# Attention couples stored in whole rows, placed by loads of squares, and gated by VectorE

## The chip, the core and the metric

The kernel runs on one core of one Trainium2 chip. A core has five instruction streams: TensorE (PE in the profile, PEld for its weight loads), VectorE (DVE), ScalarE (ACT), GpSimd (POOL) and SyncE (SP), which here only issues DMAs. Each stream runs its instructions in the order in which they were written and waits for semaphores where it is told to. The metric is device time in microseconds. The kernel before took 924.09 us (median of three runs, 919.69 to 927.16).

## The reference, cut to what matters

One decoder layer on 1024 rows of width 1024, in float32:

```python
h = rms_norm(x, pre_norm)
proj = h @ w_in                      # q, k, v, gate_a, u, v_b, gate_b, mg_a, mg_b
o_a = sliding_window_attention(q, k, v, sinks, rel_bias)   # 16 heads of 64, window 128
y_a = (o_a * silu(gate_a)) @ w_branch_a
o_b = spatial_gating(gelu(u), gelu(v_b), ...)
y_b = (o_b * silu(gate_b)) @ w_branch_b
out = (sigmoid(mg_a) * y_a + sigmoid(mg_b) * y_b) @ w_out
x = x + rms_norm(out, post_norm)
```

The change touches what lies between the softmax of the attention and the product `o_a * silu(gate_a)`. For each head and each block of 128 queries the probabilities (128 queries by 2 x 128 keys, folded into one 128 x 128 tile) have to be transposed, so that TensorE can multiply them with the values.

## The kernel before, in words

Matrices are multiplied in pieces of high and low parts (`w_hi`, `w_lo`; three matmuls for one product), and in seven products in place of eight per pair of column blocks. After a first stage (normalisation, `v_b`, keys and values; to about 137 us) come 24 pairs of column blocks, `n` = 0 to 23. Each has seven steps `s`, with one product of 12 matmuls in each. Attention is woven into steps of pairs 1 to 17: `attention_all(n, s)` turns a step into a head pair `p` (0 to 7) and a step `k` of it. A head pair begins every 14 steps and is done after 22, so that its last 8 steps lie beside the first 8 of the next. Below, "step 0" to "step 13" are the places in this period of 14 steps (about 50 us); step 16 of one head pair is step 2 of the period.

A head pair has 8 query blocks, and two blocks make a **couple** (c = 0 to 3). A couple's four 128 x 128 probability tiles lie side by side in `prob[j % 2]` (j = 4p + c). They are transposed in two parts: VectorE transposes 32 x 32 squares in place (L2143), and two sets of DMAs carry the tile out to DRAM and back, which puts the squares in their places. The stations of a couple, by the step k = 3c + lag at which each stream reaches them:

- lag 3, SP: `prob_away` stores the couple, four DMAs (L666).
- lag 4, SP: `prob_back` loads it into `turned_in`, one DMA (L675). It waits for the stores, and for GpSimd to have read the couple before out of `turned_in` (`pool_own`).
- lag 7, ACT: `turned_hi` copies it to `pt_pack` (high part, L1590).
- lag 8, POOL: the low part (L1859) and the masked copy `pt_prev` (L1864), which lets the values go.
- lag 9, PE: `values`, eight matmuls (L1073), in the middle of the step's product.
- lag 10, ACT and DVE: ACT copies two quarters of the result (L1607, L1608) to `o_tmp`, DVE adds the other two (L2149, L2150).
- lag 11, POOL: the product with the gate (L1873). SP stores the gate's row at k = 15 and 21 (L687).

In each step a stream does the attention first (`attend`) and then its part of the pair (`after`). For pair n + 1 ScalarE makes the high parts of its loaded columns (`left_hi`: L1364 for the first raw block, L1383 for half of the second, L1371 and L1378 for sums), GpSimd the low parts (`left_lo`, L1816) and the sums (L1881, L1882, L1888, L1890). SP loads the raw columns (`load_pair`, L542) at steps 5, 6, 12 and 13; they share its queue with the attention's DMAs and with the stores of the merge gates (L699).

Of the kernel before, what the change touches and what calls it, by code (L numbers as in the profile page):

```python
# [5 lines left out]
P = 128  # L6
# [13 lines left out]
HEAD_PAIRS = N_HEADS // 2  # L20
# [122 lines left out]
def build(nc, x, rel_bias, pre_norm, post_norm, w_in, sinks, sgu_ln_g, sgu_ln_b,  # L143
          w_spatial, b_spatial, w_branch_a, w_branch_b, w_out, out):
    f32 = mybir.dt.float32
# [19 lines left out]
    v_d = nc.dram_tensor("v_d", [P, 2 * NT * P], i32)  # L165
    prob_d = nc.dram_tensor("prob_d", [4 * HEAD_PAIRS, 4, P, P], f32)
    bias_d = nc.dram_tensor("bias_d", [N_HEADS, BIAS_ROW], f32)
    skew_d = nc.dram_tensor("skew_d", [N_HEADS, P, BIAS_ROW], f32)

    with ExitStack() as ctx:  # L170
# [340 lines left out]
        def _(sp):  # L511
# [150 lines left out]
            def prob_away(j):  # L662

                sp.wait_ge(turn_ok, 2 * j + 2)
                for q in range(4):
                    sp.dma_start(prob_d[j, :, :, :].rearrange("c (g a) (q b) -> q a c g b", g=4, q=4)[q],  # L666
                                 prob[j % 2][32 * q:32 * (q + 1), 1:1 + 4 * P].rearrange("a (c g b) -> a c g b", c=4, g=4)
                                 ).then_inc(prob_out[j % 2], 16)

            def prob_back(j):  # L670

                sp.wait_ge(prob_out[j % 2], 64 * (j // 2 + 1))
                if j:
                    sp.wait_ge(pool_own, POOL_FRONT + j)
                sp.dma_start(turned_in.rearrange("p (c x) -> p c x", c=4), prob_d[j, :, :, :].rearrange("c p x -> p c x")).then_inc(prob_in, 16)  # L675

            def attend(p, k):
                for c in couple_at(k, 3):
                    prob_away(4 * p + c)
                for c in couple_at(k, 4):  # L680
                    prob_back(4 * p + c)
                if k == 11 and p + 1 < HEAD_PAIRS:
                    load_bias(p + 1)
                if k in (15, 21):
                    h = k // 21
                    sp.wait_ge(og_ok, 4 * p + 2 * h + 2)
                    sp.dma_start(ga_d[bass.ds(p, 1), :, h * HALF:(h + 1) * HALF].rearrange("a p s -> p (a s)"),  # L687
                                 gate_w(p, h)).then_inc(ga_out[h], 16)
# [527 lines left out]
        def _(act):  # L1216
# [347 lines left out]
            def exps(p, blk):  # L1564
# [5 lines left out]
                if s % 2 == 0 and s >= 4:  # L1570
                    act.wait_ge(prob_out[s // 2 % 2], 64 * (s // 4))
                for h in range(2):
# [11 lines left out]
            def turned_hi(j):  # L1584
                act.wait_ge(prob_in, 16 * (j + 1))
                if j:
# [5 lines left out]
            def attend(p, k):  # L1592
# [4 lines left out]
                if k == 2 and p + 1 < HEAD_PAIRS:  # L1597
                    act.dma_start(*skew(p + 1)).then_inc(bias_out, 16)
                for c in couple_at(k, 7):
                    turned_hi(4 * p + c)  # L1600
                for g in couple_at(k, 10):
# [83 lines left out]
            for n in range(1, PAIRS):  # L1685
                for s in range(7):
                    for at in attention_all(n, s):
                        attend(*at)
                    after(n, s)
            def after_tile(f, i):  # L1690

# [27 lines left out]
        def _(pool):  # L1719
# [126 lines left out]
            def attend(p, k):  # L1846
# [9 lines left out]
                for c in couple_at(k, 8):  # L1856
# [5 lines left out]
                    if j:  # L1862
# [4 lines left out]
                        base=-1, pattern=[[0, 8], [-1, P]], channel_multiplier=1).then_inc(pt_ok, 1)  # L1867
                for g in couple_at(k, 11):
                    if g == 0:
                        pool.wait_ge(gate_ok, 2 * p + 2)  # L1870
                    part = gate_w(p, g // 2)[:, g % 2 * 256:(g % 2 + 1) * 256]
                    pool.wait_ge(oadd_ok, 4 * p + g + 1)
                    nc.gpsimd.tensor_tensor(part, o_tmp, part, ALU.mult).then_inc(og_ok, 1)  # L1873

# [55 lines left out]
        def _(dve):  # L1930
# [184 lines left out]
            def attend(p, k):  # L2115
# [29 lines left out]
                for g in couple_at(k, 10):  # L2145
# [4 lines left out]
                    nc.vector.tensor_tensor(o_tmp[64:128, :], o[64:128, 256:512], o_tmp[64:128, :],  # L2150
                                            ALU.add).then_inc(oadd_ok, 1)

            def u_mix(n):
# [441 lines left out]
```

## Time and profile before

| | us |
|---|---|
| median of three runs | 924.09 (919.69 to 927.16) |
| the profiled execution | 923.55 |
| its span, first to last instruction | 921.8 |
| PE busy | 893.6 (97%) |
| DVE, ACT, POOL busy | 629.0, 509.3, 532.4 |
| granted TensorE clock, mean | 0.993 |

The profile is of one execution. A PE that is busy 97% of the span is pipelined matmuls end to end; what is not matmul is to be looked for in its gaps. The other engines are busy for 55 to 68% of the span, but each only in its own order.

### The profile page before, as it was taken

What the parts mean: (1) busy time and instruction counts of PE and PEld (TensorE: products, weight loads), DVE (VectorE), ACT (ScalarE), POOL (GpSimd) and SP (SyncE); (2) the same over time, 40 slices, a digit from 0 to 9 for tenths busy, and PEclk for the clock granted to TensorE, in tenths of its full rate; (3) what the DMA queues carried; (4) which work ended last, traced back from release to release, by engine and by line L of the source; (5) the groups of instructions that cost most, each with busy time, mean ns of one, the idle gap of its engine ahead of it and who ended that gap; (6) DMA issues with size and microseconds to landing.
All of it is one profiled execution on the core that took longest, in us unless ns stands there. A gap on an engine that the chain in (4) does not pass through costs nothing.

```text
span 921.8 us, 12475 instructions
## 1 busy us (share of the span) xinstructions
PE 893.6 (97%) x4204; PEld 742.8 (81%) x4204; DVE 629.0 (68%) x1135; ACT 509.3 (55%) x982; POOL 532.4 (58%) x395
## 2 busy tenths in 40 slices
PE   9999999989999998989899999999999999999997
PEld 7888888878787877778787877888888888888886
DVE  6776794536455554445463679789679878989968
ACT  6654355766767676657577684344443534434563
POOL 3564237678878878687778868454452142042236
PEclk9999999999999999999999999999999999999999
DMA  8886645363645556644536474533369650335004
GB/s 298 201 198 161 230 164 149 112 158 87 165 113 143 133 145 169 181 125 112 144 93 168 115 202 141 183 103 105 101 230 372 197 205 1 118 113 225 0 1 183
DMA packets 211472, 139.29 MB, mean 151 GB/s; under 512 B 91320, under 2 KB 180432, under 8 KB 211280
## 3 DMA queue, kind: packets, MB, share of 16 engines
q1 hardware_dynamic: 209168, 135.05, 49.8%
q10 hardware_dynamic: 2240, 3.43, 1.1%
q8 instruction: 34, 0.56, 0.3%
q14 instruction: 30, 0.25, 0.1%
HBM read 98.06 MB, written 43.54 MB: 154 GB/s over the span
## 4 chain that ended last, share of the span: by engine, by line
PE 71%; POOL 9%; ACT 6%; DVE 5%; DMA 4%; issue 4%; SPq 2%; ACTq 0%; POOLq 0%; DVEq 0%
PE acc L1033 27%; PE acc L1205 11%; PE acc L886 10%; PE ps_m L1205 7%; PE ps_t L1205 7%; DMA raw<-in_w_in 4%; PE acc L976 2%; PE ps_m L1073 2%; POOL w_lo L1816 2%; PE ps_t L1050 1%; POOL pt_pack L1859 1%; SPq L666 1%; ACT soft L1573 1%; POOL pt_prev L1864 1%; DVE soft L2134 1%
## 5 line engine op out<-in xcount | busy, mean ns | idle before, releaser
L1033 PE MATMUL acc<-mv,w_hi 128*128 128x512 f32 x1344 | 348.1, 392 | 2.9 <-ACT c L1423 1.5
L1033 PEld LDWEIGHTS acc<-mv,w_hi 128*128 128x128 f32 x1344 | 247.1, 189 | 52.4 <-issue 6.3
L1033 PE MATMUL acc<-mv,w_lo 128*128 128x512 f32 x672 | 181.0, 391 | 0.0
L1816 POOL TENSOR_TENSOR w_lo<-sums,w_hi 128x1024 fp32r<-128x1024 f32 x48 | 117.0, 2439 | 85.1 <-ACT w_hi L1371 55.0
L1033 PEld LDWEIGHTS acc<-mv,w_lo 128*128 128x128 f32 x672 | 127.4, 190 | 27.8
L1816 POOL TENSOR_TENSOR w_lo<-raw,w_hi 128x1024 fp32r<-128x1024 f32 (+1 forms) x48 | 94.4, 1967 | 43.9 <-ACT w_hi L1364 32.4
L1205 PE MATMUL acc<-right,left 128*128 128x512 f32 x432 | 98.7, 389 | 0.0
L1205 PEld LDWEIGHTS acc<-right,left 128*128 128x128 f32 x432 | 81.0, 188 | 17.2 <-DVE left L2194 0.4
L2149 DVE TENSOR_TENSOR soft<-ps_m,soft 64x256 f32<-64x256 f32 x32 | 13.3, 416 | 103.8 <-ACT soft L1608 103.8
L1573 ACT ACTIVATE soft<-soft,neg_max 128x129 f32<-128x129 f32 x128 | 50.5, 396 | 55.3 <-DVE neg_max L2134 55.2
L886 PE MATMUL acc<-mv 128*128 128x512 f32 x288 | 69.3, 395 | 0.0
L1205 PE MATMUL ps_t<-right,left 128*128 128x512 f32 x288 | 67.2, 389 | 0.0
L1205 PE MATMUL ps_m<-right,left 128*128 128x512 f32 x288 | 67.2, 389 | 0.0
L2143 DVE STREAM_TRANSPOSE soft<-soft 128x128 f32<-128x128 f32 x128 | 32.3, 292 | 50.8 <-ACT soft L1581 50.6
L1581 ACT ACTIVATE soft<-soft,inv_den 128x128 f32<-128x128 f32 x128 | 44.3, 393 | 34.9 <-DVE inv_den L2123 34.9
L1205 PEld LDWEIGHTS ps_t<-right,left 128*128 128x128 f32 x288 | 54.1, 188 | 11.2
L1205 PEld LDWEIGHTS ps_m<-right,left 128*128 128x128 f32 x288 | 54.1, 188 | 11.2
L886 PEld LDWEIGHTS acc<-mv 128*128 128x128 f32 x288 | 53.4, 188 | 11.4 <-ACT mv L1238 0.3
L1859 POOL TENSOR_TENSOR pt_pack<-soft,pt_pack 128x512 fp32r<-128x512 f32 x32 | 41.9, 1309 | 19.6 <-ACT pt_pack L1590 19.6
L1073 PE MATMUL ps_m<-pt_pack,v_st 128*128 128x256 f32 x128 | 27.1, 305 | 17.6 <-POOL pt_prev L1864 17.6
L1073 PEld LDWEIGHTS ps_m<-pt_pack,v_st 128*128 128x128 f32 x128 | 21.1, 198 | 25.5 <-POOL pt_prev L1864 24.0
L2134 DVE CUSTOM_DVE_ANT_0 soft<-ps_t,bias_t,sink_b 128x128 f32<-128x128 f32 x128 | 39.9, 350 | 2.1
(282 smaller groups left out, 1661.5 us busy)
## 6 DMA issues: line engine op xcount, KB each, us to landing
raw<-in_w_in SPq DMA_DIRECT2D x56, 512.0 KB, 5.3
prob_d<-soft SPq DMA_DIRECT2D x128, 64.0 KB, 3.5
soft<-prob_d SPq DMA_DIRECT2D x32, 256.0 KB, 3.1
ht_d<-sums SPq DMA_DIRECT2D x8, 512.0 KB, 5.2
mix_d<-mix_b SPq DMA_DIRECT2D x8, 512.0 KB, 3.8
ga_d<-gate SPq DMA_DIRECT2D x16, 256.0 KB, 4.6
tb<-tb_d SPq DMA_DIRECT2D x4, 1024.0 KB, 5.3
ub<-mix_d SPq DMA_DIRECT2D x7, 512.0 KB, 3.5
```

The source lines that it names most:

```text
L886: ins = nc.tensor.matmul(acc[b][:, hf * HALF:(hf + 1) * HALF], left, right, start=(m < 2), stop=(m >= 46), skip_group_check=True)
L976: ins = nc.tensor.matmul(acc[b][:, hf * HALF:(hf + 1) * HALF], (w_lo if x == 2 else w_hi)[:, w], right, start=(m < 2), stop=(m >= 46), ski ...
L1033: ins = nc.tensor.matmul(bank, (w_lo if y == 2 else w_hi)[:, left + k * P:left + (k + 1) * P], right[:, (OPW if y == 1 else 0) + k * HALF: ...
L1073: ins = nc.tensor.matmul(o, v_st[:, v0:v0 + P], pt[:, y * 512:(y + 1) * 512].rearrange("p (x c) -> p x c", x=4)[:, heads, :], start=(kb == ...
L1205: ins = nc.tensor.matmul(bank, l[:, c:c + P], r[:, (OPW if y == 1 else 0) + k * HALF:(OPW if y == 1 else 0) + (k + 1) * HALF], start=(m == ...
L1573: ins = nc.scalar.activation(exp_w(s, h), neg_w(blk, h), ACT.Exp, scale=-1.0, bias=neg_max[:, head(blk, h)], accum_out=row_sum[:, head(blk ...
L1581: ins = nc.scalar.activation(w, w, ACT.Copy, scale=inv_den[:, head(blk, h)])
L1816: nc.gpsimd.tensor_tensor(w_lo[:, c], src, w_hi[:, c].bitcast(f32), ALU.subtract).then_inc(wlo_ok, 1)
L1859: nc.gpsimd.tensor_tensor(pt_pack[:, 512:1024], turned_in, pt_pack[:, 0:512].bitcast(f32), ALU.subtract).then_inc(pool_own, 1)
L2134: ins = nc.vector.tensor_tensor_reduce(out=neg_w(blk, h)[:, 1 - h:1 - h + P], in0=bank[:, h * 256 + P:(h + 1) * 256], in1=bias_t[:, bias:b ...
L2143: ins = nc.vector.transpose(w, w)
L2149: own.link(nc.vector.tensor_tensor(o_tmp[0:64, :], o[0:64, 0:256], o_tmp[0:64, :], ALU.add))
```

## The change

`prob_d` now has one row of 512 numbers for each of 128 partitions. `prob_away` stores a couple with one DMA of whole rows (2 KB each), and `prob_back` loads it with four, one for each group of 32 partitions, whose pieces are rows of squares (32 numbers, 128 bytes): the squares are placed on the way back and not on the way out. `prob_back` moves from lag 4 to lag 5, and the gate's stores from k = 15 and 21 to 14 and 20. On ACT `turned_hi` keeps its lag of 7 but now stands behind `after` of its step, where it stood ahead of the copies and of `after`. The product with the gate is made by VectorE at lag 10, right behind the addition, and no longer by GpSimd at lag 11.

```diff
-    prob_d = nc.dram_tensor("prob_d", [4 * HEAD_PAIRS, 4, P, P], f32)
+    prob_d = nc.dram_tensor("prob_d", [4 * HEAD_PAIRS, P, 4 * P], f32)
...
-                for q in range(4):
-                    sp.dma_start(prob_d[j, :, :, :].rearrange("c (g a) (q b) -> q a c g b", g=4, q=4)[q],
-                                 prob[j % 2][32 * q:32 * (q + 1), 1:1 + 4 * P].rearrange("a (c g b) -> a c g b", c=4, g=4)
-                                 ).then_inc(prob_out[j % 2], 16)
+                sp.dma_start(prob_d[j, :, :], prob[j % 2][:, 1:1 + 4 * P]).then_inc(prob_out[j % 2], 16)
...
-                sp.wait_ge(prob_out[j % 2], 64 * (j // 2 + 1))
+                sp.wait_ge(prob_out[j % 2], 16 * (j // 2 + 1))
                 if j:
                     sp.wait_ge(pool_own, POOL_FRONT + j)
-                sp.dma_start(turned_in.rearrange("p (c x) -> p c x", c=4), prob_d[j, :, :, :].rearrange("c p x -> p c x")).then_inc(prob_in, 16)
+                for g in range(4):
+                    sp.dma_start(turned_in[32 * g:32 * (g + 1), :].rearrange("a (c q b) -> a c q b", c=4, q=4),
+                                 prob_d[j, :, :].rearrange("(q a) (c g b) -> g a c q b", q=4, c=4, g=4)[g]).then_inc(prob_in, 16)
...
-                for c in couple_at(k, 4):
+                for c in couple_at(k, 5):
                     prob_back(4 * p + c)
...
-                if k in (15, 21):
-                    h = k // 21
+                if k in (14, 20):
+                    h = k // 20
...
-                for c in couple_at(k, 7):
-                    turned_hi(4 * p + c)
...
                     after(n, s)
+                    for p, k in attention_all(n, s):
+                        for c in couple_at(k, 7):
+                            turned_hi(4 * p + c)
...
-                for g in couple_at(k, 11):
-                    if g == 0:
-                        pool.wait_ge(gate_ok, 2 * p + 2)
-                    part = gate_w(p, g // 2)[:, g % 2 * 256:(g % 2 + 1) * 256]
-                    pool.wait_ge(oadd_ok, 4 * p + g + 1)
-                    nc.gpsimd.tensor_tensor(part, o_tmp, part, ALU.mult).then_inc(og_ok, 1)
...
+                    dve.wait_ge(oadd_ok, gg + 1)
+                    if g == 0:
+                        dve.wait_ge(gate_ok, 2 * p + 2)
+                    part = gate_w(p, g // 2)[:, g % 2 * 256:(g % 2 + 1) * 256]
+                    nc.vector.tensor_tensor(part, o_tmp, part, ALU.mult).then_inc(og_ok, 1)
```

Three places show how instructions move (the lines of the changed kernel are one to six lower). The first is ScalarE's order at step 2 of the period, where the fourth couple (c = 3) is turned. Before:

```order
L1456 ACTIVATE ev<-ev 128x512
L1590 ACTIVATE pt_pack<-soft 128x512
L1607 ACTIVATE soft<-ps_m 64x256
L1608 ACTIVATE soft<-ps_m 64x256
L1581 ACTIVATE soft<-soft,inv_den 128x128 x2
L1598 DMA skew_d<-bias_d 256x1x384
L1451 ACTIVATE ev<-ev 128x512
L1383 ACTIVATE w_hi<-raw 128x512
```

and now:

```order
L1455 ACTIVATE ev<-ev 128x512
L1604 ACTIVATE soft<-ps_m 64x256
L1605 ACTIVATE soft<-ps_m 64x256
L1580 ACTIVATE soft<-soft,inv_den 128x128 x2
L1597 DMA skew_d<-bias_d 256x1x384
L1450 ACTIVATE ev<-ev 128x512
L1382 ACTIVATE w_hi<-raw 128x512
L1589 ACTIVATE pt_pack<-soft 128x512
```

The copy to `pt_pack` has gone from the head of this stretch to its end. The second place is ScalarE at step 7, where the first couple (c = 0) is turned. Before:

```order
L1573 ACTIVATE soft,row_sum<-soft,neg_max 128x129 x2
L1590 ACTIVATE pt_pack<-soft 128x512
L1468 ACTIVATE ev<-ev 128x512
L1364 ACTIVATE w_hi<-raw 128x1024
L1581 ACTIVATE soft<-soft,inv_den 128x128 x2
```

and now:

```order
L1572 ACTIVATE soft,row_sum<-soft,neg_max 128x129 x2
L1467 ACTIVATE ev<-ev 128x512
L1363 ACTIVATE w_hi<-raw 128x1024
L1589 ACTIVATE pt_pack<-soft 128x512
L1580 ACTIVATE soft<-soft,inv_den 128x128 x2
```

Here two instructions come between, and the second of them reads a raw block from DRAM. The third place is SP's order over steps 3 to 6 (with what each DMA waits for). Before:

```order
L666 DMA prob_d<-soft 32x16x32 [waits turn_ok]
L666 DMA prob_d<-soft 32x16x32 x3
L675 DMA soft<-prob_d 128x4x128 [waits pool_own,prob_out0]
L699 DMA tb_d<-c 128x512 [waits mt_ok]
L542 DMA raw<-in_w_in 128x8x128 [waits wlo_ok,sum_ok]
```

and now:

```order
L665 DMA prob_d<-soft 128x512 [waits turn_ok]
L673 DMA soft<-prob_d 32x16x32 [waits pool_own,prob_out0]
L673 DMA soft<-prob_d 32x16x32 x3
L698 DMA tb_d<-c 128x512 [waits mt_ok]
L542 DMA raw<-in_w_in 128x8x128 [waits wlo_ok,sum_ok]
```

The load of the first raw block still stands behind the couple's round trip; what was four DMAs and one is now one and four. Behind it (step 6) the next couple's stores, four before and one now, stand ahead of the second raw block's load.

## Rows read from the trace of the kernel before

**Rows 1.** The page: engines by busy us, share of the span, instructions.

```profile
PE   893.6 (97%) x4204; PEld 742.8 (81%) x4204; DVE 629.0 (68%) x1135; ACT 509.3 (55%) x982; POOL 532.4 (58%) x395
```

**Rows 2.** Waits: who waited for whom, us in total, times, longest.

```profile
PE ps_m L1073 <- POOL pt_prev L1864: 17.6, 15, 2.8
```

**Rows 3.** Timeline, PE's values, couples 1, 3, 0, 1 (start, us, [idle before]).

```profile
251.12 0.51 PE L1073 MATMUL ps_m<-pt_pack,v_st 128*128 128x256 f32 x2 [1.53 <-POOL pt_prev L1864]
...
421.08 0.40 PE L1073 MATMUL ps_m<-pt_pack,v_st 128*128 128x256 f32 x2
...
437.76 0.74 PE L1073 MATMUL ps_m<-pt_pack,v_st 128*128 128x256 f32 x4 [0.50 <-POOL pt_prev L1864]
...
450.46 0.68 PE L1073 MATMUL ps_m<-pt_pack,v_st 128*128 128x256 f32 x2 [2.41 <-POOL pt_prev L1864]
```

**Rows 4.** Timeline of GpSimd between the first couple and the second.

```profile
441.58 1.30 POOL L1881 TENSOR_TENSOR sums<-raw 128x512 f32<-128x512 f32 x1 [1.51 <-issue]
```

**Rows 5.** Timeline of ScalarE at step 2, fourth couple.

```profile
415.47 0.62 ACT L1590 ACTIVATE pt_pack<-soft 128x512 fp32r<-128x512 f32 x1
...
418.04 0.40 ACT L1581 ACTIVATE soft<-soft,inv_den 128x128 f32<-128x128 f32 x1 [1.14 <-DVE inv_den L2123]
...
419.22 0.62 ACT L1383 ACTIVATE w_hi<-raw 128x512 fp32r<-128x512 f32 x1
```

**Rows 6.** Timeline of ScalarE at step 7, first couple.

```profile
434.08 0.62 ACT L1590 ACTIVATE pt_pack<-soft 128x512 fp32r<-128x512 f32 x1
434.60 0.62 ACT L1468 ACTIVATE ev<-ev 128x512 f32<-128x512 f32 x1
436.25 1.06 ACT L1364 ACTIVATE w_hi<-raw 128x1024 fp32r<-128x1024 f32 x1 [1.04 <-DMA raw<-in_w_in]
```

**Rows 7.** Timeline, third couple, GpSimd idle till ScalarE's copy: ScalarE, GpSimd, PE.

```profile
254.97 0.63 ACT L1590 ACTIVATE pt_pack<-soft 128x512 fp32r<-128x512 f32 x1
...
257.05 1.09 POOL L1864 TENSOR_SCALAR_AFFINE_SELECT pt_prev<-pt_pack 128x1024 fp32r<-128x1024 f32 x1
...
260.82 0.40 PE L1073 MATMUL ps_m<-pt_pack,v_st 128*128 128x256 f32 x2
```

**Rows 8.** Timeline, fourth couple three head pairs earlier: ScalarE, then PE.

```profile
265.32 0.62 ACT L1590 ACTIVATE pt_pack<-soft 128x512 fp32r<-128x512 f32 x1
...
270.93 0.40 PE L1073 MATMUL ps_m<-pt_pack,v_st 128*128 128x256 f32 x2
```

**Rows 9.** Chain of waits (start, us): PE behind the second couple and the third.

```profile
450.46 1.96 PE ps_m L1073 x8
452.43 6.31 PE acc L1033 x24
...
461.93 0.95 PE ps_m L1073 x8
...
463.35 5.46 PE acc L1033 x24
```

**Rows 10.** Windows: length, busy of PE, PEld, DVE, ACT, POOL, clock, DMA, GB/s.

```profile
451.00:453.00 2.00, 2.00 (x9) 1.89 (x9) 0.00 (x0) 0.00 (x0) 2.00 (x2) 0.50 1.09 272
252.00:254.00 2.00, 2.00 (x11) 1.68 (x11) 0.00 (x0) 0.25 (x1) 2.00 (x1) 1.00 1.13 261
```

**Rows 11.** Timeline of SP's queue: the raw blocks' loads of steps 5 and 6.

```profile
430.34 0.38 SPq L542 DMA_DIRECT2D raw<-in_w_in  x1
...
435.99 0.40 SPq L542 DMA_DIRECT2D raw<-in_w_in  x1
```

**Rows 12.** Lines of DVE: duration ns min/median/max, first and last start.

```profile
L2109 DVE SCALAR_TENSOR_TENSOR gate<-c x8: 681/1508/1532, 163.8 to 509.8; 128x512 f32<-128x512 f32 x8
...
L2149 DVE TENSOR_TENSOR soft<-ps_m,soft x32: 407/417/419, 196.4 to 572.4; 64x256 f32<-64x256 f32 x32
```

**Rows 13.** DMA issues: count, KB each, median us from issue to landing.

```profile
prob_d<-soft SPq DMA_DIRECT2D x128, 64.0 KB, 3.5
...
ta_d<-ev SPq DMA_DIRECT2D x8, 256.0 KB, 2.0
```

More of the change, by code:

```diff
@@ L1570, in exps @@
                 if s % 2 == 0 and s >= 4:
-                    act.wait_ge(prob_out[s // 2 % 2], 64 * (s // 4))
+                    act.wait_ge(prob_out[s // 2 % 2], 16 * (s // 4))
                 for h in range(2):
@@ L1584, in turned_hi @@
             def turned_hi(j):
-                act.wait_ge(prob_in, 16 * (j + 1))
+                act.wait_ge(prob_in, 64 * (j + 1))
                 if j:
```

## The prediction

> **What bounds the kernel now.** Read the page first. PE is busy for 893.6 us, 97% of the span of 921.8 [rows 1], so at most 28.2 us are to be had from waits, and what matters is what PE waits for. The waits name one thing: PE stood 17.6 us in 15 waits before the values of the attention, for GpSimd's `pt_prev` [rows 2]. The timeline of PE shows where. In each period of 14 steps the first couple (c = 0) waits some 0.5 us and the second (c = 1) 1.5 to 2.4 us; the fourth (c = 3) does not wait, and neither does the third [rows 3]. Over the eight head pairs I take 3.3 us for the first couples (six of 0.50 to 0.53 and one of 0.16), 0.8 us for the last fourth couple, and so 13.5 us for seven second couples.
>
> Two more things are needed. First, from the first couple's values to the point at which PE wants the second's is 10.3 us (450.46 − 2.41 − 437.76), whereas GpSimd was on its way from the one to the other for 12.7 us, of which it stood 1.51 us at L1881 until a raw block had landed [rows 3, 4]. Its own work there is thus 11.2 us, 0.9 us more than PE leaves it: of a second couple's wait 0.9 us is GpSimd's work, and the rest is the late load. Second, in the chain of waits PE takes 1.96 us for eight values matmuls and 6.31 us for the 24 behind them after a wait of 2.41 us, where the third couple shows 0.95 and 5.46 [rows 9]: 1.9 us lost again. The windows show why. The granted clock is 0.50 behind that wait, the 1.2 GHz level, and 1.00 behind one of 1.53 us [rows 10]. Three of the seven second couples waited 2.4 us or more: 3 x 1.9 = 5.6 us.
>
> **ScalarE's order.** This is the part with a cost. ScalarE's time of the turned copy stands at a fixed distance from PE: in the fourth couple 5.61 us before the values, at 415 us as at 265 us [rows 3, 5, 8]. So I can reckon each couple alone. From the start of the copy to the end of `pt_prev`, where GpSimd has nothing else to do, it takes 3.17 us (257.05 + 1.09 − 254.97) [rows 7].
>
> Fourth couple. The copy began at 415.47 and PE wanted the values at 421.08: 2.4 us to spare. Now it comes behind L1383, which ended at 419.84 [rows 5]. The copy's own 0.62 us is gone from ahead of it, and VectorE's product comes into the path, since the reciprocal for which L1581 waits [rows 5] stands behind it on DVE. The product is 128 x 256. It costs at least the 0.42 us of the addition L2149, and at most the 1.51 us of L2109, which is twice as wide; I take 0.5, the nearest in size being L2149 [rows 12]. The copy begins at 419.6, `pt_prev` ends at 422.8, and PE waits 1.7 us where it waited not at all. Eight times this is 13.6 us, less the 0.8 us of the last one before: **+12.8 us**.
>
> First couple. The copy began at 434.08; PE was ready at 437.26 and waited 0.50 us [rows 3, 6]. Now L1468 and L1364 come first: 0.52 + 0.97 us as they overlap, if the raw block is there. The copy begins at 435.57, `pt_prev` ends at 438.74, and PE waits 1.48 us. Eight times is 11.8 less 3.3: **+8.5 us**.
>
> Second couple. The copy now stands behind the two small copies and one eviction; GpSimd, with its 11.2 us of work, comes to it at about the same time. Third couple: the two small copies and L1378 come first, and PE takes the values 5.85 us after the old start of the copy (260.82 − 254.97) [rows 7], of which 3.17 are needed. **0** for both, with a few tenths open for the second.
>
> **The round trip.** A couple's 256 KB went out in four DMAs of 64 KB in pieces of 128 bytes, 3.5 us to landing each. Whole rows of 2 KB are what the store of `ta_d` makes of the same 256 KB: 2.0 us [rows 13]. The way back takes over the 2048 small pieces, which no row shows for this tensor; by the nearest, the old stores, 3.5 us after the last issue, with 2.0 us as the lower end. `prob_back` leaves a step later (3.6 us, 199.3 us between two second couples over 56 steps [rows 3]), yet ScalarE wants the couple later too, by 1.5 us in the first couple and 4.1 in the fourth. I cost it at 0 on the couple's own path. Its cover is the distance from lag 5 to the end of lag 7; where that is gone, all later instructions on ScalarE stand behind `prob_in`.
>
> What the trip gives is on SP's queue. The first raw load (430.34) stood behind a `prob_back` that waited for slow stores, the second (435.99) behind four stores [rows 11]. Now the first stands behind four loads, but the store ahead lands sooner; the second behind one store. I take the second raw block to land before GpSimd is at L1881 (2 us or more earlier, where 1.51 was missing). Each second couple then waits only GpSimd's own 0.9 us: 8 x 0.9 = 7.2 in place of 13.5, **−6.3 us**. No wait is then over 1.7 us, and the clock stays up: **−5.6 us**.
>
> **The gate.** GpSimd loses 32 products, yet in the stretch that sets the second couple's wait, from one `pt_prev` to the next, it made none: 0. VectorE's product at steps 10, 13 and 5 stands ahead of a reciprocal as well, but there ScalarE's two copies now come 0.6 us earlier or the path has slack of over 1 us: 0. Behind the waiting DVE stand c22, the q parts and the transposes, none of which PE waits for within a step.
>
> A rule speaks against this part. The row first: L2109, with both inputs in SBUF, takes 0.68 us at its quickest and 1.51 at the median, while GpSimd is at work beside it [rows 12]. The Trainium skill, in "SBUF — State Buffer", section "Who interferes with whom", says that a VectorE instruction with two SBUF inputs shares an exclusive lock with GpSimd's reads, and that the other "fully blocks". By it the product could stand for one whole GpSimd instruction. The sum takes the product at 0.5 because GpSimd has just ended its sums at step 2 and now stands until the copy comes.
>
> **Sum.** 12.8 + 8.5 − 6.3 − 5.6 = +9.4 us on the profiled execution's 923.55: **933 us**. That execution lies 0.5 us under the median of the runs, 924.09, which changes nothing at this precision. About 1% is what a measurement of this kernel can tell from no change, that is 915 to 933.
>
> **Rivals.** (1) *The copies' places don't matter* and only the gains remain: 923.55 − 6.3 − 5.6 = 912 us, faster. It holds if ScalarE, no longer held by late loads, runs ahead of PE by more than 1.7 us. For it: ScalarE is busy for 55% of the span. Against it: the fixed 5.61 us, which the late load of one period and not of another left alone. (2) *One of the two new waits is covered*, most likely the first couple's (924 us, +0.9) or the fourth's (920 us): no change. Half a microsecond less on the path, or GpSimd's work in front of `pt_prev` in place of ScalarE, would do it for part. (3) *The raw block is late for ScalarE.* Before, L1364 stood 1.04 us for it, and nobody else did, because the turned copy was ahead [rows 6]. Now the copy is behind it, so each microsecond by which that load is late goes to PE, eight times. With the same 1.04 us: 933 + 8 = 941 us; from about 2 us on, the wait exceeds 2.4 us and 1.9 us of low clock are added each time. (4) *VectorE's product is held* for 1.5 us where I took 0.5: 8 us, 941 us. By the page's rule, one whole GpSimd subtraction, the same mechanism would show a product of over 2 us. (5) *The clock falls behind the new waits*: 1.7 us lies between 1.53, where it stayed, and 2.41, where it fell. At the eight fourth couples that is 8 x 1.9 = 15 us, 948 us. (6) *The stores don't get quicker* since what slows them is other traffic; the second couple's 6.3 and the clock's 5.6 us are not gained: 945 us.
>
> **Chances.** The forecast (927 to 939) 0.45; rivals 3 to 6 together (939 to 950) 0.23; rival 2 (919 to 927) 0.17; rival 1 (909 to 917) 0.15. The range leaves out most of rival 1 and the far end of 3 to 6: 915 to 945. Slower by over 1% (above 933) is half of the forecast and all of 3 to 6: 0.46. Within 1%: the other half and rival 2: 0.39. Faster by over 1%: 0.15.
>
> **What would show it.** In the profile after: PE's values of fourth couples with a wait of 1.7 us, first couples with 1.5, second couples with 0.9, all named as GpSimd's; GpSimd's L1859 waiting for ScalarE's copy at fourth couples by over 3 us; L1881 without a wait for its load; no window at clock 0.50 in the attention; the gate's product on DVE at 0.4 to 0.6 us. I would be wrong if the copy's distance to PE's values has grown at steps 2 or 7 by other ways than its place, if `prob_in` holds ScalarE, or if L1881 still waits.

## The result and the profile after

The changed kernel took 952.7 us (median of four runs, 951.8 to 955.8) beside 925.6 for the kernel before (919.7 to 928.7): a ratio of 1.0306, 95% interval 1.0248 to 1.0365. It is slower by 3%. The forecast was 933, with a range of 915 to 945: the direction was right, but the size was a third of what came, and the result lies outside the range. The two profiled executions took 923.55 and 952.93 us, 29.4 apart where 9.4 were forecast.

The page of the changed kernel, engines by busy us, share and instructions (against [rows 1]):

```profile
PE   903.0 (95%) x4204; PEld 750.7 (79%) x4204; DVE 644.5 (68%) x1167; ACT 508.0 (53%) x982; POOL 510.0 (54%) x363
```

The same 4204 matmuls are busy for 9.4 us longer. The work is the same, and the windows below show the granted clock at half in more stretches. The rest is waiting. The waits of the changed kernel (against [rows 2]):

```profile
PE ps_m L1072 <- POOL pt_prev L1864: 38.8, 23, 2.4
```

So there are 38.8 us of waits for `pt_prev` where there were 17.6. The time in which PE is not busy at all (span less busy) went from 28.2 to 48.2 us, and 20.0 + 9.4 make the 29.4. The timeline of PE's values, fourth couple, first, second, fourth (start, us, [idle before]):

```profile
388.19 0.50 PE L1072 MATMUL ps_m<-pt_pack,v_st 128*128 128x256 f32 x2 [1.94 <-POOL pt_prev L1864]
...
407.40 0.74 PE L1072 MATMUL ps_m<-pt_pack,v_st 128*128 128x256 f32 x4 [1.34 <-POOL pt_prev L1864]
...
418.74 0.51 PE L1072 MATMUL ps_m<-pt_pack,v_st 128*128 128x256 f32 x2 [1.21 <-POOL pt_prev L1864]
...
441.12 0.51 PE L1072 MATMUL ps_m<-pt_pack,v_st 128*128 128x256 f32 x2 [2.42 <-POOL pt_prev L1864]
```

The fourth couples wait 2.40 to 2.43 us six times and 1.94 once (1.7 forecast), the last not at all; the first 1.18 to 2.27 (1.48 forecast); the second 0.99 to 1.23 (0.9 forecast); the third not at all. The path to the last of these rows is best read from the end. ScalarE, VectorE and GpSimd before 441.12:

```profile
435.81 0.40 ACT L1580 ACTIVATE soft<-soft,inv_den 128x128 f32<-128x128 f32 x1 [1.48 <-DVE inv_den L2117]
...
437.52 0.62 ACT L1589 ACTIVATE pt_pack<-soft 128x512 fp32r<-128x512 f32 x1
```

```profile
427.97 2.62 DVE L2103 SCALAR_TENSOR_TENSOR gate<-c 128x512 f32<-128x512 f32 x1
430.51 0.15 DVE L2117 RECIPROCAL inv_den<-row_sum 128x2 f32<-128x2 f32 x1
...
435.28 0.42 DVE L2150 TENSOR_TENSOR gate<-soft,gate 128x256 f32<-128x256 f32 x1
435.62 0.16 DVE L2117 RECIPROCAL inv_den<-row_sum 128x2 f32<-128x2 f32 x1
...
438.10 0.69 DVE L2103 SCALAR_TENSOR_TENSOR gate<-ev 128x512 f32<-128x512 f32 x1
```

```profile
427.63 2.41 POOL L1816 TENSOR_TENSOR w_lo<-sums,w_hi 128x1024 fp32r<-128x1024 f32 x1
430.00 2.85 POOL L1816 TENSOR_TENSOR w_lo<-raw,w_hi 128x1024 fp32r<-128x1024 f32 x1
...
438.21 1.70 POOL L1859 TENSOR_TENSOR pt_pack<-soft,pt_pack 128x512 fp32r<-128x512 f32 x1 [2.87 <-ACT pt_pack L1589]
```

ScalarE's copy (L1589) starts 1.18 us before PE is ready (441.12 − 2.42 = 438.70). Beside its new place, which was the forecast's reason, three things make it and what follows late. The product (L2150) takes 0.42 us ahead of a reciprocal, and ScalarE waits 1.48 us for that where it was 1.14 [rows 5]: this was foreseen. GpSimd's L1859 takes 1.70 us where it takes 1.29 elsewhere, with VectorE's `gate<-ev`, two inputs in SBUF, beside it: this was not. And `gate<-c` takes 2.62 us. It starts 0.34 us behind a GpSimd subtraction and ends 0.55 us after it (427.97 + 2.62 = 430.59; 427.63 + 2.41 = 430.04).

The same trace has one fourth couple, at 388.19, ahead of which `gate<-c` is not held:

```profile
375.44 0.68 DVE L2103 SCALAR_TENSOR_TENSOR gate<-c 128x512 f32<-128x512 f32 x1
```

There the product starts 3.91 us before PE is ready and not 3.43, and the wait is 1.94 us and not 2.42: the held `gate<-c` is worth 0.48 us of each such wait.

The clock behind the waits, in windows of the changed kernel (columns as in [rows 10]):

```profile
460.70:463.70 3.00, 3.00 (x9) 2.32 (x9) 2.60 (x8) 1.49 (x6) 3.00 (x3) 0.50 0.76 223
441.40:443.40 2.00, 2.00 (x16) 1.87 (x16) 0.50 (x2) 0.00 (x0) 2.00 (x2) 1.00 0.13 51
```

It is at 0.50, the 1.2 GHz level, in nine stretches of 3.4 us in the attention, where the kernel before had three. Four of them begin within 1.3 us of a fourth couple's wait (1.94 to 2.42 us) and five at a first couple's (1.79 to 2.27); behind the wait of 2.42 us at 441 the clock stayed at 1.00, as behind two more of that size. The round trip's loads land after 2.7 us, inside the forecast's 2.0 to 3.5. Its stores land after 3.4 us where 2.0 were forecast. It never held ScalarE here. DMA issues: count, KB each, median us to landing (against [rows 13]):

```profile
prob_d<-soft SPq DMA_DIRECT2D x32, 256.0 KB, 3.4
soft<-prob_d SPq DMA_DIRECT2D x128, 64.0 KB, 2.7
```

### The profile page after: what moved, and what is told of

The parts are those of the page before. It is cut to its first block, busy times and chain, and to the rows that moved or that the text cites. A ratio compares the mean times of both kernels' runs of the same rounds, so it can differ in the third digit from the quotient of the medians.

```text
span 951.2 us, 12475 instructions
## 1 busy us (share of the span) xinstructions
PE 903.0 (95%) x4204; PEld 750.7 (79%) x4204; DVE 644.5 (68%) x1167; ACT 508.0 (53%) x982; POOL 510.0 (54%) x363
## 3 DMA queue, kind: packets, MB, share of 16 engines
q10 hardware_dynamic: 2240, 3.43, 1.0%
## 4 chain that ended last, share of the span: by engine, by line
PE 63%; POOL 14%; issue 9%; ACT 6%; DVE 5%; DMA 2%; SPq 1%; POOLq 0%; ACTq 0%; DVEq 0%
PE acc L1032 21%; PE acc L1204 10%; PE acc L885 9%; PE ps_m L1204 7%; PE ps_t L1204 7%; POOL w_lo L1816 5%; POOL pt_pack L1859 3%; POOL pt_prev L1864 3%; PE acc L975 2%; PE ps_m L1072 2%; DMA raw<-in_w_in 2%; PE ps_t L1049 2%; ACT soft L1572 1%; ACT w_hi L1370 1%; DVE soft L2128 1%
## 5 line engine op out<-in xcount | busy, mean ns | idle before, releaser
L1032 PEld LDWEIGHTS acc<-mv,w_hi 128*128 128x128 f32 x1344 | 249.7, 190 | 47.7 <-issue 0.3
L1032 PE MATMUL acc<-mv,w_lo 128*128 128x512 f32 x672 | 184.3, 397 | 0.0
L1032 PEld LDWEIGHTS acc<-mv,w_lo 128*128 128x128 f32 x672 | 129.9, 193 | 28.8
L1859 POOL TENSOR_TENSOR pt_pack<-soft,pt_pack 128x512 fp32r<-128x512 f32 x32 | 45.4, 1419 | 66.7 <-ACT pt_pack L1589 66.7
L1072 PE MATMUL ps_m<-pt_pack,v_st 128*128 128x256 f32 x128 | 28.0, 312 | 38.8 <-POOL pt_prev L1864 38.8
L2125 DVE COPY_PREDICATED ps_t<-before,ps_t 128x256 f32<-128x256 int32 x56 | 23.8, 425 | 59.8 <-PE ps_t L1049 59.4
```

The source lines that it names most:

```text
L1032: ins = nc.tensor.matmul(bank, (w_lo if y == 2 else w_hi)[:, left + k * P:left + (k + 1) * P], right[:, (OPW if y == 1 else 0) + k * HALF: ...
L1072: ins = nc.tensor.matmul(o, v_st[:, v0:v0 + P], pt[:, y * 512:(y + 1) * 512].rearrange("p (x c) -> p x c", x=4)[:, heads, :], start=(kb == ...
L1859: nc.gpsimd.tensor_tensor(pt_pack[:, 512:1024], turned_in, pt_pack[:, 0:512].bitcast(f32), ALU.subtract).then_inc(pool_own, 1)
L2125: own.link(nc.vector.copy_predicated(blocks(bank)[:, :, 1, :], before_i, blocks(bank)[:, :, 0, :]))
```

## The experiments

Times are medians; each ratio is to the kernel before on the same chip, with its 95% interval. Each trace is of one execution, and the clock differs between executions of one kernel (mean 0.979 to 0.985 in the change's four). "Ahead" and "behind" are the places of ScalarE's copy.

### The three parts one by one

**a3_trip_only**: kernel before with the new round trip alone. 

> The kernel before with the new trip alone (whole rows out, squares placed by four loads, a step later); copy at its old place, product on GpSimd, gate's stores at their old steps. Theory: the second raw block no longer holds GpSimd's sums, 912 to 918 us, within 3 us of the kernel that has the product on VectorE as well. Rival (trip costs): slower than 924 us.

**b1_copy_behind**: kernel before with the copy behind `after`. 

> The kernel before with ScalarE's turned copy behind the step's own work and nothing else changed. Theory: this alone makes it slower than the full change or as slow, 948 to 962 us: fourth couples wait some 1.6 us (no VectorE product ahead of the reciprocal), first couples 1.8 us and up to 1 us more since the raw block is still late for L1364, second couples 1.5 us and more, and the clock falls in most periods. Rival (the order is covered, trip or gate is the cost): within 5 us of the kernel before.

**b2_gate_vector**: kernel before with the product on VectorE. 

> The kernel before with the product with the gate on VectorE behind its addition and nothing else changed. Theory: the product takes 0.43 us and is off the path; GpSimd had no product in the stretch that makes PE wait, so within 3 us of the kernel before (921 to 928 us). Rival (gate is the cost): 935 us or more.

**a1_copy_ahead**: changed kernel with one part undone:

```diff
+                for c in couple_at(k, 7):
+                    turned_hi(4 * p + c)
                 for g in couple_at(k, 10):
...
                     after(n, s)
-                    for p, k in attention_all(n, s):
-                        for c in couple_at(k, 7):
-                            turned_hi(4 * p + c)
```

> The changed kernel with ScalarE's turned copy back at its old place, ahead of the copies of the values and of the step's own work; trip and gate as changed. Theory (ScalarE's order is the cost): fourth couples wait for nothing, first couples 0.5 us, second couples 0.9 to 1.2 us, the clock does not fall in the attention; 912 to 918 us, faster than the kernel before. Rival (the trip with loads of squares is the cost): the copy waits for prob_in, and the time stays at 940 us or more. Rival (VectorE's product is the cost): also 940 or more, with the waits of VectorE's reciprocal longer.

| | us | ratio |
|---|---|---|
| before | 924.8 | |
| trip | 917.1 | 0.9899 (0.987 to 0.9929) |
| copy behind | 939.1 | 1.013 (1.0079 to 1.0181) |
| product on VectorE | 935.5 | 1.0095 (1.0051 to 1.0139) |
| trip + product (a1) | 933.1 | 1.0084 (1.0059 to 1.011) |
| trip + copy behind + product (the change) | 952.7 | 1.0306 (1.0248 to 1.0365) |

The trip alone is faster, the copy costs 14 us, and the product on VectorE, which the forecast had at 0 on its own, costs 11 to 16. The expectations that rested on a free product (a1, b2, and a3's "within 3 us" of a1) fell. So did b1's 948 to 962: its fourth couples wait 1.61 us, as expected, but most of its first couples 1.18 and not 1.8, its second couples 1.04 and not 1.5, and the clock falls twice. Two of its first couples wait 2.85 and 4.44 us, where ScalarE stood 1.59 and 3.18 us for the raw block just before. Where the product's price arises is seen in b2 at step 5, VectorE and GpSimd:

```profile
277.86 1.01 DVE L2150 TENSOR_TENSOR gate<-soft,gate 128x256 f32<-128x256 f32 x1
278.80 0.15 DVE L2117 RECIPROCAL inv_den<-row_sum 128x2 f32<-128x2 f32 x1
```

```profile
276.20 2.40 POOL L1816 TENSOR_TENSOR w_lo<-sums,w_hi 128x1024 fp32r<-128x1024 f32 x1 [2.42 <-ACT w_hi L1371]
```

The product ends at 278.87, 0.27 us after GpSimd's subtraction (278.60); ScalarE waits 2.07 us for the reciprocal where it waited 1.14, and the first couple's copy starts 1.53 us before PE is ready where a3 shows 3.16.

### Is it the place, or what VectorE reads?

**a7_product_psum**: a1 with another input of the product. It leaves the addition out of what is multiplied, so that one input lies in PSUM.

```diff
-                    nc.vector.tensor_tensor(part, o_tmp, part, ALU.mult).then_inc(og_ok, 1)
+                    nc.vector.tensor_tensor(part, o[:, 0:256], part, ALU.mult).then_inc(og_ok, 1)
...
-                    pe.wait_ge(oadd_ok, g - 1)
+                    pe.wait_ge(og_ok, g - 1)
```

> As the kernel with the copy ahead and the product on VectorE behind the addition (933.1), but the product reads the first 256 columns of the values' bank in PSUM in place of o_tmp, so that one input lies in SBUF and one in PSUM; TensorE waits for the product before it writes that bank again. (What is computed is changed: it multiplies the gate with numbers before the addition.) Theory A with the lock of two SBUF inputs: the products take 0.42 us each and not 1.0 at the mean (32.0 us in all), the normalisation at step 5 waits 1.5 us in place of 2.07, and the time lies between 917 and 933, about 924. Rival E, the product is long for another reason (its place, its shape): 32 us of products, and 933.

It took 918.5 us, 0.9934 (0.9905 to 0.9963), which leaves 1.4 us (by the ratios 3) of the 16 between a1 and a3. VectorE's group of products in a1, then in a7 (busy us, mean ns):

```profile
L2149 DVE TENSOR_TENSOR gate<-soft,gate 128x256 f32<-128x256 f32 x32 | 32.0, 999 | 1.1
```

```profile
L2149 DVE TENSOR_TENSOR gate<-ps_m,gate 128x256 f32<-128x256 f32 x32 | 13.6, 424 | 1.1
```

And at step 5 of a7 the product stands in the middle of the same subtraction of GpSimd and takes 0.42 us (VectorE, GpSimd):

```profile
425.50 0.42 DVE L2149 TENSOR_TENSOR gate<-ps_m,gate 128x256 f32<-128x256 f32 x1
```

```profile
423.83 2.40 POOL L1815 TENSOR_TENSOR w_lo<-sums,w_hi 128x1024 fp32r<-128x1024 f32 x1 [2.42 <-ACT w_hi L1370]
```

So a VectorE instruction of two SBUF inputs stands until GpSimd's ends, and one of the same size with one input in PSUM doesn't. With the copy ahead this is nearly the whole price of the product. The length of a held one is regular: in the kernel before, the change, b2, a1, a5, a6, a10 and a13, each of the 117 products of over 0.9 us ends 0.27 to 0.29 us after the GpSimd instruction beside which it started, and each of the 25 such `gate<-c` 0.55 us after it.

**a8_sum_in_psum** makes the whole computation in this way: the additions write to PSUM.

```diff
-                    own.link(nc.vector.tensor_tensor(o_tmp[0:64, :], o[0:64, 0:256], o_tmp[0:64, :], ALU.add))
-                    nc.vector.tensor_tensor(o_tmp[64:128, :], o[64:128, 256:512], o_tmp[64:128, :],
+                    own.link(nc.vector.tensor_tensor(o[0:64, 0:256], o[0:64, 0:256], o_tmp[0:64, :], ALU.add))
+                    nc.vector.tensor_tensor(o[64:128, 0:256], o[64:128, 256:512], o_tmp[64:128, :],
```

> Copy ahead, new round trip, product on VectorE behind the addition; but the addition leaves its result in PSUM (the first 256 columns of the values' bank) and the product reads it there, with the gate in SBUF: the whole computation is made, and no product has two inputs in SBUF. TensorE waits for the product before it writes that bank again. Theory A with the lock: like the kernel whose product read PSUM without the sum, 918.5, so 916 to 921, products of 0.42 us each, none longer. Rival F: writing sums to PSUM or holding the bank for the product makes TensorE wait: 925 or more.

921.6 us, 0.997 (0.9948 to 0.9991), products of 0.42 us: the mechanism as expected, the time at the end of its range. Its first couples wait 1.21 us.

**a6_ahead_late** (a1 with the product at the end of VectorE's step) and **a5_product_late** (the same on the changed kernel):

```diff
                     after(n, s)
+                    for p, k in attention_all(n, s):
+                        for g in couple_at(k, 10):
...
+                            nc.vector.tensor_tensor(part, o_tmp, part, ALU.mult).then_inc(og_ok, 1)
```

> The changed kernel with ScalarE's copy ahead as before and VectorE's product at the end of VectorE's step. The same with the product behind the addition took 933.1, and with the product on GpSimd 917.1. Theory A: ScalarE's normalisation at step 5 waits 1.14 us again and not 2.07, the first couples' copy is 3.1 us before PE's values and not 1.53, their waits go from 2.14 to about 0.5 us: 8 x 1.6 = 13 us less and 3 stretches at low clock (6 us), 916 to 921. Rival D, load or port wherever it stands: 930 to 935.

> The changed kernel with VectorE's product moved from behind the addition to the end of VectorE's step (behind its part of the pair). Theory A: the reciprocal comes 0.37 us earlier, so the fourth couples wait 2.0 in place of 2.42 us; gate<-c still takes 2.6 us, because GpSimd's work is where it was. With 8 x 0.37 = 3 us less and the falls of the clock behind these waits partly gone (up to 8 us), 941 to 950. Rival D, it is the mere load on VectorE or the shared port, wherever the product stands: 952 +- 3.

a6: 925.0 us, 0.9977 (0.9947 to 1.0007), a gain over a1 of half of what was expected: its first couples still wait 1.75 us, and its products are still long (25.9 us in all), only in another place. a5: 940.7 us, 1.0149 (1.0096 to 1.0201), with fourth couples at 2.2 us and `gate<-c` at 2.9. Neither theory's numbers hold for a6. Place and lock seem to pay a part each; a6 does not separate them, since the late product is held too.

**a12_psum_late**: a8 with the product at the end of the step. 

> As the kernel before in this list, with the product at the end of VectorE's step. In the one with the product behind the addition, the first couples waited 1.02 us where they wait 0.5 with the product on GpSimd; theory A says that this is the product's own 0.42 us ahead of the reciprocal, so that it goes: 0.5 us at each of 7 first couples, 914 to 918. Rival D, the product is now beside GpSimd's work wherever it stands and costs the same: 918 to 921, no different.

 920.5 us, 0.9962 (0.994 to 0.9985), first couples at 0.98 us: theory A missed, and the time is the one that rival D gave. The place of an unheld product is worth about 1 us here, which the noise hardly tells from nothing, and why the first couples wait 0.98 and not the 0.5 of a3 stays open.

### The same in the changed kernel: a lock whose victim changes

**a2_gate_gpsimd**: changed kernel with the product back on GpSimd at lag 11. 

> The changed kernel with one part undone: the product with the gate is back on GpSimd at lag 11 (the gate's row stored at k = 15 and 21); the new round trip and the copy behind stay. Theory A, the product on VectorE costs time because it stands ahead of the reciprocal for which ScalarE's normalisation waits, and because GpSimd without its product comes to its big subtraction earlier, beside VectorE's gate<-c (2.62 us in the trace of the change, 0.87 in that of the kernel with the copy behind alone). Then the fourth couples wait 1.6 us as in that kernel, gate<-c takes under 1 us, there is at most one stretch at clock 0.50, and the time is 931 to 939 us, at least 14 less than the change's 952.7. Rival B, the costs of the parts don't depend on each other (-7.7 for the trip, +14 for the copy, +11 for the product): 925 + 14 - 8 = 931. Rival C, the copy behind is what costs once the trip is new: it stays at 948 or more.

935.7 us, 1.0105 (1.0043 to 1.0167). The product on VectorE thus costs 17 us in the changed kernel (19 by the ratios). In its trace the fourth couples wait 1.61 us, no stretch of the attention is at low clock, and PE is busy for 888.9 us, 14.1 less than in the change. The spans are 20.3 us apart, so the clock is the larger part. The traced execution is a2's fastest (932.67 us, mean clock 0.999); two of the other three, at 0.991 and 0.994, took 939.3 and 937.7 us, so in these the clock was down for longer. B (931) lies inside the interval and can't be told apart by this run alone; but the three parts added up (−7.7, +14.2, +10.7) would put the change at 942, and it stood at 952.7. The 2.4 in its waits is one first couple, behind a late raw block, and the clock stayed up behind it:

```profile
PE ps_m L1072 <- POOL pt_prev L1864: 30.7, 23, 2.4
```

**a9_behind_psum**: the changed kernel with the two edits of a8. 

> The changed kernel (copy behind) with the sum left in PSUM and the product reading it there. At the fourth couples the change's product was 0.42 us long already; what was long there was gate<-c, 2.62 us, held by GpSimd's subtraction that had moved up. Theory A: so little is gained, the fourth couples wait 2.2 to 2.4 us, gate<-c stays at 2.6, 943 to 952. Rival G: in the changed kernel, too, the products' lock is the whole cost of the product, as with the copy ahead: 935 to 939, like the kernel with the product on GpSimd (935.7).

 941.5 us, 1.0183 (1.0131 to 1.0235), between the two expectations. The fourth couples wait 2.4 us and `gate<-c` takes 2.48 as A said, but the clock falls four times and not nine, and the first couples wait 1.18 to 1.72 us. The products took 19.0 us in the change and 13.6 here. What is shorter is mostly the product at step 5, which took 1.00 to 1.11 us in the change, beside a subtraction, and stands ahead of the next first couple's copy. These 5.4 us, and what they did to the clock, were worth 11 us.

**a10_stand_in**: the changed kernel with GpSimd's time for a product put back.

```diff
+                for g in couple_at(k, 11):
...
+                    b2 = before[:, None, :].to_broadcast([P, 2, P])
+                    nc.gpsimd.tensor_tensor(ident[:, :].bitcast(bf16).rearrange("p (h j) -> p h j", h=2), b2, b2,
+                                            ALU.mult).then_inc(idle_ok, 1)
```

> The changed kernel, and at lag 11, where GpSimd made the product before, it makes a stand-in of the same width (0.7 us, constants, its result unused). VectorE's product stays. Theory A's second half (GpSimd without its product comes 1.1 us earlier to its subtraction, which then holds VectorE's gate<-c for 2.6 us): gate<-c falls under 1 us, the fourth couples wait 2.0 us, and a kernel with more work is faster: 938 to 946. Rival H, gate<-c is not on the path: 952 or more.

959.4 us, 1.0381 (1.0332 to 1.0429): theory A is wrong in the time and right in its first step. The time is rival H's; a11 below shows that `gate<-c` is on the path all the same. VectorE, then GpSimd, of a10 ahead of a fourth couple:

```profile
483.33 0.68 DVE L2110 SCALAR_TENSOR_TENSOR gate<-c 128x512 f32<-128x512 f32 x1
...
490.16 1.40 DVE L2157 TENSOR_TENSOR gate<-soft,gate 128x256 f32<-128x256 f32 x1
```

```profile
484.03 2.40 POOL L1817 TENSOR_TENSOR w_lo<-sums,w_hi 128x1024 fp32r<-128x1024 f32 x1
...
490.00 1.28 POOL L1883 TENSOR_TENSOR sums<-raw 128x512 f32<-128x512 f32 x1
```

`gate<-c` is over before the subtraction starts and takes 0.68 us. But against PE, GpSimd is 1.0 us later at this subtraction and 0.6 us at its last sum, and the product, no longer delayed by `gate<-c`, starts 0.5 us earlier. So this sum now meets the product, which took 0.42 us in the change and takes 1.40 here. The fourth couples wait 2.91 us.

**a11_stand_in_psum**: a10 and a9 together. 

> The changed kernel with both edits together: the stand-in of the product's width on GpSimd, and the product on VectorE reading its sum from PSUM. With the stand-in alone gate<-c fell from 2.62 to 0.68 us, but then the product at the fourth couples stood beside GpSimd's sum and took 1.40 us (959.4 us); with PSUM alone the products took 0.42 us but gate<-c 2.5 (941.5 us). Theory A, one lock whose victim changes: with both, neither is long, the fourth couples wait 2.0 us (1.61 with the product on GpSimd, and its 0.4 on VectorE), 936 to 940 us. Rival I, the stand-in costs by GpSimd's own time: 945 or more.

 941.7 us, 1.0167 (1.0149 to 1.0186). VectorE, then PE:

```profile
472.25 0.68 DVE L2110 SCALAR_TENSOR_TENSOR gate<-c 128x512 f32<-128x512 f32 x1
...
478.95 0.42 DVE L2157 TENSOR_TENSOR gate<-ps_m,gate 128x256 f32<-128x256 f32 x1
```

```profile
484.81 0.76 PE L1073 MATMUL ps_m<-pt_pack,v_st 128*128 128x256 f32 x2 [1.96 <-POOL pt_prev L1865]
```

Neither is long, and the wait is the 2.0 us of theory A; the time is 2 us above its range, with the clock at 0.50 four times where a2's trace had none.

The fourth couples of these kernels lie on one line: the wait is 5.43 us less the time from the end of the product ahead of ScalarE's reciprocal to the point at which PE is ready. That time is 3.01 us in the change (wait 2.42), 3.49 in its one period with a free `gate<-c` (1.94), 2.51 in a10 (2.91) and 3.47 in a11 (1.96).

### The places of the four couples

**a4_two_ahead**: changed kernel, the copy ahead for the first and fourth couple. 

> The changed kernel with ScalarE's copy ahead for the first and the fourth couple, and behind for the second and the third. The prediction cost the places of the second and the third at 0: then as with all four ahead, 931 to 935. If the second and third couples' places cost something too, 937 or more.

**a13_fourth_behind**: changed kernel, the copy behind for the fourth alone. 

> The changed kernel with the copy behind for the fourth couple alone. The step from all ahead (933.1) to all behind (952.7) is 19.6 us. The prediction gave the fourth couples 12.8 and the first 8.5 us; by that split and the low clock behind waits of 2.4 us, 946 to 950. If the first couples, whose copies are 1.5 us late already with VectorE's product in front, are the larger part: 936 to 941.

```diff
                         for c in couple_at(k, 7):
-                            turned_hi(4 * p + c)
+                            if c == 3:
+                                turned_hi(4 * p + c)
```

a4 took 941.1 us, 1.0168 (1.0143 to 1.0193); a13 940.6, 1.0151 (1.0122 to 1.0179). Both miss what the prediction's terms gave; each lies in the range of its second expectation. PE's values in a4 (first couple, second) and in a13 (fourth, first):

```profile
447.28 0.84 PE L1072 MATMUL ps_m<-pt_pack,v_st 128*128 128x256 f32 x4 [2.54 <-POOL pt_prev L1868]
...
459.97 0.50 PE L1072 MATMUL ps_m<-pt_pack,v_st 128*128 128x256 f32 x2 [1.00 <-POOL pt_prev L1868]
```

```profile
481.69 0.50 PE L1072 MATMUL ps_m<-pt_pack,v_st 128*128 128x256 f32 x2 [2.58 <-POOL pt_prev L1868]
...
498.94 0.74 PE L1072 MATMUL ps_m<-pt_pack,v_st 128*128 128x256 f32 x4 [0.96 <-POOL pt_prev L1868]
```

In a4 the third couples don't wait and each second couple waits about 1.0 us, 8.2 us in all where a1 has 4.1. The first couples, whose copies are ahead, wait 2.34 to 2.58 us where a1 shows 2.14 to 2.37, the clock falls seven times and not four, and the kernel is 8 us over a1. `gate<-c` is held again, but the fourth couples behind it don't wait, and what makes the first couples later than a1's is not shown. VectorE's group in a4:

```profile
L2107 DVE SCALAR_TENSOR_TENSOR gate<-c 128x512 f32<-128x512 f32 x8 | 17.4, 2170 | 0.0
```

In a13 the fourth couples' 2.58 us are new. `gate<-c` takes 0.68 us there, but the product ahead of them is held for 1.07 us and ends 2.84 us before PE is ready, on the line above. In the one period in which it takes 0.42 us the wait is 1.94. The first couples' wait falls from a1's 2.14 to 0.96: while PE stands at one couple the other engines catch up for the next. Waits in one period are not a sum of independent terms.

## Why the prediction was wrong, point by point

The forecast was +9.4 us on the profiled execution, and 29.4 came. Waits for `pt_prev` were forecast at 13.6 + 11.8 + 7.2 = 32.6 us (fourth, first, second couples); they are 16.5 + 13.6 + 8.8 = 38.8: 6.2 more. Matmul time was forecast at −5.6 us and is +9.4: 15.0 more. PE's other idle time fell from 10.6 to 9.4 us, 1.2 less. 6.2 + 15.0 − 1.2 are the 20.0 us that were missing.

- **The clock (−5.6): the step that failed.** It rested on "no wait is then over 1.7 us". The waits grew: twelve of them are 1.79 to 2.43 us, the clock fell at nine of the twelve, and matmul time rose by 9.4 us where it was to fall by 5.6. Rival 5, falls behind the new waits, has the right mechanism, and its 15 us are in part luck: it had eight falls, all at fourth couples, and there were four there and five at first couples. a2's trace shows the other side: fourth couples at 1.61 us, no fall in the attention, 888.9 us of matmuls. Nor does the term come with the trip alone: a3's trace has 893.2 us of matmuls and three falls, one at a wait of 2.83 us for `ps_t`, which the forecast didn't look at, one at a second couple's 1.91 us and one at the last fourth couple's 2.50. The forecast also gave 948 us to a rival and yet ended its range at 945.
- **Fourth couples (1.7 us each; 2.42 measured).** The working without the product gave 1.2; b1 and a2 measure 1.61, because GpSimd's L1859 takes 1.70 us and not 1.29 beside `gate<-ev`, so that it is 3.56 us and not 3.17 from the copy's start to the end of `pt_prev`. The product's own place adds 0.35 (1.96 in a11), near the 0.5 taken. The lock on `gate<-c` adds the last 0.46 (2.42). Rival 4, the product itself held for 1.5 us there, didn't come: it took 0.42. The last fourth couple, priced at 1.7, didn't wait.
- **First couples (1.48 each; 1.18 to 2.27, mean 1.70).** With the product on GpSimd they wait mostly 1.18 (a2), less than forecast. What is above that goes with the product at step 5, held for 1.0 us in the change, for which the forecast had "slack of over 1 us"; with it at 0.42 they wait 1.18 to 1.39 but for the last (a9). ScalarE's copy of the raw block (L1363 now) stood for its DMA twice in the whole kernel, neither time beside the attention's values, so rival 3 didn't come.
- **Second couples (0.9; 0.99 to 1.23), third (0), trip (0 on its own path).** Right in size. The successor of L1881 stood for no load beside the attention's values, and with the trip alone (a3) six of the second couples wait 0.82 to 0.89 us. But the −6.3 is not the trip's gain in the change: in b1, with the old trip and the copy behind, the second couples already wait only 0.98 to 1.33 us, 8.5 in all, and from b1 to a2 the trip is worth 3 us where it is worth 8 alone. Rival 6 had its condition and not its price: the stores got no quicker (3.5 us a quarter before; whole, 3.4 in the change and 4.2 in a3), and the second couples' gain came in a3 all the same. In a3 the trip did hold ScalarE's copy once, for 2.27 us, at the last third couple, whose values then waited 0.26 us. And "0 for the places of the second and third" is wrong in effect: a4 shows 8 us.
- **The gate (0): wrong by 11 to 17 us, by the ratios up to 19.** It was reckoned from its own 0.42 us and the slack beside it. The rule cited in the prediction was the right one: first the rows, the product is 1.01 us beside GpSimd's subtraction and 0.42 us beside the same subtraction with one input in PSUM. The Trainium skill, "SBUF — State Buffer", "Who interferes with whom", says that two SBUF inputs contend with a GpSimd instruction that reads SBUF and that an instruction with one does not; this case agrees with both. The error was to apply it to the product at one place, ahead of the fourth couples (where, at 0.42 us, it was indeed not held in the change). It was not asked what GpSimd does beside the product at step 5, nor which other VectorE instruction GpSimd's work would meet once GpSimd had lost 0.7 us per couple. That was `gate<-c`: 1.51 us before [rows 12], 0.87 in a2 and mostly in b1, 2.62 in the change.

What stays open: why the clock fell behind some waits of 2.42 us and not behind others (all seven of 2.34 to 2.58 us in a4, one of six of 2.58 in a13, none behind one of 2.41 in a2 or one of 2.53 in a7), and so why a11 and a2, 0.35 us apart in a wait, are 6 us apart in time.

## What to carry to other kernels

Before an elementwise instruction is moved between GpSimd and VectorE, list every VectorE instruction with two SBUF inputs on the critical chain and look at what GpSimd does beside it before and after: the move also shifts all later work of the engine that loses it, and another pair may collide. If one input can be left in PSUM, that instruction's collision is gone, as in a8. When a tuned kernel's waits come near the size behind which the trace shows the clock falling, price the falls as the likely case, and read waits within a period as one budget.

## What the runs showed that was not expected

- The exclusion works in both directions. VectorE's two-input instructions of 0.42 and 0.68 us take up to 2.62 and 2.91 (both in a5), ending 0.27 to 0.55 us after GpSimd's; GpSimd's 1.29 us L1859 takes 1.70 where VectorE's instruction of 0.69 us starts 0.11 us before it, and its subtraction 2.85 in place of 2.41 beside `gate<-c`.
- Whole rows of 2 KB gained little: one store of 256 KB lands after 3.4 us, four of 64 KB after 3.5, though `ta_d` of the same size and shape needs 2.0 [rows 13]. It stands beside other traffic; this was not taken apart.
- The best version is the trip alone (a3), 917.1 us, 0.9899 (0.987 to 0.9929). None of those with the product on VectorE, held or not, beats it.
